# ScalarE's order in the first feed-forward projection: the gate slab's split ahead of Silu

## The reference

```
def swiglu_ffn(h, w_in, w_out):            # h: 256 x 1024
    gate, up = jnp.split(h @ w_in, 2, axis=-1)     # w_in: 1024 x 5632
    return (jax.nn.silu(gate) * up) @ w_out        # w_out: 2816 x 1024

x = x + 0.5 * swiglu_ffn(rms_norm(x, gain), w_in, w_out)
```

## Time and profile before

| | |
|---|---|
| times of three runs, us | 2641.64, 2650.41, 2651.55 |
| span of the profiled execution, us | 2652.8 |
| mean granted clock of PE in it | 0.992 |
| PE busy | 2573.4 us, 97% |
| VectorE busy | 1748.1 us, 66% |
| ScalarE busy | 1318.0 us, 50% |
| moved by DMA | 424.27 MB, mean 160 GB/s |
| `lo` on VectorE (L347) | 728 of them, 936.0 us |
| `hi` on ScalarE (L339) | 728 of them, 784.8 us |
| Silu (L692) | 176 of them, 73.5 us |

### The profile page before, as it was taken

The page is one execution under the profiler, slowest core; times in us unless marked ns, Lnnn a source line. Parts: engine busy times, 40 slices in busy tenths (PEclk is TensorE's granted clock), DMA queues, the critical chain, the costliest instruction groups (busy, mean ns, idle before and its releaser), DMA issues.

```text
span 2652.8 us, 60759 instructions
## 1 busy us (share of the span) xinstructions
PE 2573.4 (97%) x23370; PEld 2508.3 (95%) x23370; DVE 1748.1 (66%) x2814; ACT 1318.0 (50%) x1974; POOL 74.6 (3%) x106
## 2 busy tenths in 40 slices
PE   8998998899999999999999999899999999999999
PEld 7997977899999999989999999899999999999999
DVE  5757566566656757767657757967667566665774
ACT  5544433355545546545535547455455455554653
POOL 0000342000000000000000000000000000000000
PEclk9999999999999999999999999999999999999999
DMA  5654201344555655445654655236656564552564
GB/s 193 202 194 134 96 3 42 112 150 152 194 192 174 204 192 204 146 143 176 201 178 144 210 175 192 73 113 204 205 173 201 191 181 131 151 144 88 190 206 143
DMA packets 114323, 424.27 MB, mean 160 GB/s; under 512 B 12433, under 2 KB 19044, under 8 KB 113796
## 3 DMA queue, kind: packets, MB, share of 16 engines
q1 hardware_dynamic: 105696, 408.99, 46.3%
q10 hardware_dynamic: 8484, 13.30, 2.4%
HBM read 421.12 MB, written 1.12 MB: 159 GB/s over the span
## 4 chain that ended last, share of the span: by engine, by line
PE 91%; DVE 4%; ACT 2%; issue 1%; DMA 0%; ACTq 0%; POOL 0%; SPq 0%; DVEq 0%; POOLq 0%
PE bank L470 21%; PE bank L471 21%; PE bank L472 21%; PE bank L396 5%; PE bank L398 4%; PE bank L397 4%; PE bank L2268 2%; PE bank L1684 1%; PE bank L1659 1%; ACT hi L339 1%; PE bank L451 1%; PE bank L452 1%; PE bank L453 1%; PE bank L1230 1%; PE bank L1668 1%
## 5 line engine op out<-in xcount | busy, mean ns | idle before, releaser
L347 DVE TENSOR_TENSOR lo<-raw,hi 128x1024 fp32r<-128x1024 f32 (+1 forms) x728 | 936.0, 1294 | 396.7 <-ACT hi L339 395.2
L339 ACT ACTIVATE hi<-raw 128x1024 fp32r<-128x1024 f32 (+1 forms) x728 | 784.8, 1106 | 338.9 <-PE bank L398 194.5
L470 PE MATMUL bank<-Hh,hi 128*128 128x256 f32 x3056 | 849.5, 278 | 4.6 <-DVE lo L347 4.5
L471 PE MATMUL bank<-Hl,hi 128*128 128x256 f32 x3056 | 848.8, 278 | 0.0
L472 PE MATMUL bank<-Hh,lo 128*128 128x256 f32 x3056 | 848.7, 278 | 0.0
L470 PEld LDWEIGHTS bank<-Hh,hi 128*128 128x128 f32 x3056 | 577.8, 189 | 6.7 <-DVE lo L347 5.7
L471 PEld LDWEIGHTS bank<-Hl,hi 128*128 128x128 f32 x3056 | 574.7, 188 | 0.0
L472 PEld LDWEIGHTS bank<-Hh,lo 128*128 128x128 f32 x3056 | 574.5, 188 | 0.0
L471 PE MATMUL bank<-Al,hi 128*128 128x256 f32 x1408 | 390.5, 277 | 0.0
L472 PE MATMUL bank<-Ah,lo 128*128 128x256 f32 x1408 | 390.5, 277 | 0.0
L470 PE MATMUL bank<-Ah,hi 128*128 128x256 f32 x1408 | 390.4, 277 | 0.0
(11 more groups left out here) (418 smaller groups left out, 4158.7 us busy)
## 6 DMA issues: line engine op xcount, KB each, us to landing
raw<-in_w SPq DMA_DIRECT2D x600, 512.0 KB, 3.4
raw<-in_w SPq DMA_DIRECT2D x128, 704.0 KB, 4.3
dB<-dil_bias ACTq DMA_DIRECT2D x16, 384.0 KB, 9.4
X<-in_x SPq DMA_DIRECT2D x2, 512.0 KB, 5.4
mem_x<-in_mem ACTq DMA_DIRECT2D x1, 1024.0 KB, 5.0
gWS<-in_ws ACTq DMA_DIRECT2D x1, 1024.0 KB
gBS<-in_bs ACTq DMA_DIRECT2D x1, 1024.0 KB
out_x<-X SPq DMA_DIRECT2D x4, 256.0 KB, 2.6
```

What stands on the lines that cost most here:

```text
L339: act.activation(k.hi[:, q, :w], k.raw[:, q, :w], ACT.Copy).then_inc(k.hi_ready, 1)
L347: dve.tensor_tensor(k.lo[:, q, :w], k.raw[:, q, :w], k.hi[:, q, :w].bitcast(F32), ALU.subtract).then_inc(k.lo_ready, 1)
L470: pe.matmul(out, wh, xh, start=first, stop=False)
L471: pe.matmul(out, wh, xl, start=False, stop=False)
```

## The change

In ScalarE's order of a pair, the split of the next gate slab stands ahead of the waits for the scaled gate, and so ahead of Silu. Its own waits (the slab has landed, PE is through with the buffer) go with it. No other engine's order is touched.

```
                 turn = st.base // RING + i + 1
+                sh.act_hi(act, s + RING, 2 * j, ahead, turn)
                 act.wait_ge(k.gate_scaled, g + 1)
                 act.wait_ge(k.a_ready, g + 1)
                 act.activation(k.sgate[:, j, :], k.gate[:, j, :], ACT.Silu).then_inc(k.silu_done, 1)
-                sh.act_hi(act, s + RING, 2 * j, ahead, turn)
                 sh.act_hi(act, s + 1 + RING, 2 * j + 1, ahead, turn)
                 act.wait_ge(k.a_ready, g + 3)
```

## The result

| | kernel before | changed kernel |
|---|---|---|
| median of 15 runs each, us | 2655.34 (2641.64 to 2668.72) | 2666.07 (2657.12 to 2677.36) |
| ratio | | 1.0043, 95% interval 1.0024 to 1.0062 |
| span of the profiled execution, us | 2652.8 | 2662.3 |
| mean granted clock in it | 0.992 | 0.989 |

In these 30 runs the changed kernel is 0.2 to 0.6% slower; 0.3% was forecast. The kernel before was timed again in each of four later sessions.

The account below looks back on a forecast made before the run. PE, busy 97% of the span, was taken as the bound. Stall -1.5, clock -1.7, small waits -0.9 and paces +11.6 sum to +7.5 us: 2652.8 becomes 2660.3 profiled, 2658 as median, range 2643 to 2667.

Parts of the forecast that it names:

- the second case: Stage 0 draws the slow pace after its 0.74 us wait, paces carried: another 6.7 us, 2664.5; chance 0.17.
- The stall: PE's wait ahead of slab 4 in stage 0 shrinks by 1.51 us, from 2.25 to 0.74 us.
- Rival (d): ScalarE stays idle behind its table load, so stage 0's wait shrinks by only 0.32 us: 2649 to 2661; chance 0.04.
- The clock: Behind stage 0's wait, the half-speed stretch from about 34.9 to 38.3 goes: 1.7 us won.
- Later pairs: After a stage's first pair, VectorE's turn falls from 5.26 to 3.75 us, under PE's 5.44; nothing lost.
- The small waits: PE's waits at slab 4 of stages 1 to 7 vanish: 0.9 us won.
- The paces: Without waits at slab 4, feed-forward blocks keep the pace their norm gave, 276 or 281 ns per matmul: +11.6 us.
- The toggle: The norm matmuls in a stage's first pair of slabs switch PE between 276 and 281 ns, without an exception.
- rival (b): Paces carried, and stage 0 draws the slow one after its 0.74 us wait: another 6.7 us, 2664.5; chance 0.17.
- rival (c): Paces carried, but draws at waits upstream (1181, 1403, 2469 us) fall otherwise, one or two blocks quicker: 2651 or 2644; chance 0.14.
- The baseline: Two of the eight feed-forward blocks of the kernel before run slow, at 0.1178 us per matmul; median 2650.4 us.
- Rival (a): Pace isn't carried, or is drawn evenly at unseen places, so only the waits count: 2646 us; chance 0.23.

Follow-up runs that it names:

- run 3: New order in all pairs of each stage but the first, against the kernel before: 2656.53 against 2658.02 us, ratio 0.9987.
- run 1: The kernel before, unchanged, profiled once more: one execution 2669 us, median of 29 runs 2658 us.
- run 8: Kernel before with the new order in stage 0 only and one extra float32 matmul behind slab 7 there: 2668.23 us, ratio 0.9992.
- run 10: The kernel before, unchanged, profiled a third time in the last session: 2672.54 us (23 runs).
- run 2: New order in the first pair of each stage alone, against the kernel before: 2669.89 against 2658.02 us, ratio 1.0054.
- run 4: Changed kernel with one more float32 matmul ahead of slab 4 in stages 1 to 7: 2663.36 us, ratio to the kernel before 1.0035.
- run 7: Changed kernel with one extra float32 matmul in each of stages 0, 2, 4 and 7: 2663.33 us, ratio to the kernel before 0.9962.
- run 12: Changed kernel with extra float32 matmuls in stages 0, 2, 4 and 7, timed again: 2656.56 us, ratio to the kernel before 0.9941.
- run 6: Changed kernel, stages 1 to 7: PE waits for itself ahead of slab 4, then one float32 matmul: 2673.23 us, ratio to the kernel before 1.0034.

## Why the prediction was right, and where it wasn't

The direction, the size and the mechanism came out in the session of the result: forecast +7.5 us in the profiled pair, measured +9.5; median forecast 2658, measured 2666, just inside the range and near the second case's 2664.5. Of the 8 us between these medians 4.9 are the kernel before's own: its median was 2650.4 in three runs and 2655.3 in 15. That +7.5 came so near to +9.5 is partly luck, as the parts show.

- **The stall**: -1.51 forecast, -1.51 measured (34.35 to 32.84). The drain behind the table load that the Trainium skill has (ScalarE: Activation LUTs, What ACT_TABLE_LOAD costs) isn't there: the split starts at 30.05, 0.01 us behind the load's end at 30.04. Rival (d) is out by the same line.
- **The clock**: full speed from 34.95 to 38.30, as forecast, and 1.5 us there where 1.7 was forecast. Over the 14 profiles a half-speed stretch followed the stall in two of four with 2.25 us of waiting and in none of ten with 0.7 us. It bought nothing that the span shows. Elsewhere the changed kernel lost some 6 us in and beside half-speed stretches (0.989 against 0.992 on the mean), a part that the sum doesn't have; the drops differ from execution to execution.
- **Later pairs cost nothing**: shown by run 3, within its interval. VectorE's turn of 3.75 us was exact.
- **The small waits** are gone in stages 1 to 7: the steps to slab 4's first matmul are 0.9 us shorter together, as worked out, and the steps behind it another 0.4.
- **The paces**: +11.6 us forecast, +7.9 measured. The eight blocks gave +13.1 of the 13.4 forecast, and the streams between them -5.2 where -1.8 was forecast. These 3.7 us less and the clock's 6 us more offset each other in part, and that is the luck in the sum.
- **The toggle** held at twelve norms of each of the 14 profiles, 168 of 168. The other four of each profile (27.6, 206.4, 490.1 and 1394.2 in the profile before) have idle matmuls or other kinds of matmuls behind them, and no toggle can be read there: the "without an exception" of the prediction covers the streams.
- **The term that went the other way** is stage 0. I let it draw quick; behind the 0.7 us wait it came slow in 9 of 10 profiles, behind the 2.25 us one in 1 of 4. That is 6.5 us in the profiled pair, rival (b), to which I gave 0.17. It was hidden there, since the upstream draws, as in rival (c), went one block the other way: stages 5, 6 and 7 were slow, quick, quick instead of quick, slow, slow. The count of four slow blocks was the forecast's, the places were not; that it agreed is luck.
- **The baseline**: I took two slow blocks for the kernel before's own. Three more profiles with its waits had three, three and four, and its median in other sessions was up to 17 us higher. Its lead of 0.4% goes with sessions in which its draws at slab 4 fell well (13 of 21 quick in the profiles of the earlier trace rows, runs 1 and 3); in the last two sessions (5 of 14 quick in runs 8 and 10) there was no lead. Five profiles are few for that, and it is argued from them rather than shown. What the 14 profiles do show is that the paces make most of the spread between executions: the spans differ by 33 us, and less 4.5 ns for each step at the slow pace (6726 to 11864 of them, steps of 116 to 120 ns) by 12. A forecast of the mean over sessions would have been nearer to no change.
- Rival (a), that no pace is carried, is out by runs 2 and 4. The Trainium skill (TensorE: Matmul & The Clock Gate, Back-to-back issue gap) gives about 81 ns at 128 columns and 131 ns at 512 for a stream of weight loads and matmuls, and nothing for 256; its N/2.4 + 2.5 ns, 109 ns at 256, is for an isolated matmul. It has no second pace, and 113.3 and 117.8 ns are neither's number.

What the paces are inside PE stays open, and so does why stage 0 falls slow behind the shorter wait.

## What to carry to other kernels

When one engine is busy for 97%, look at the start-to-start step of its instructions and not at its waits alone: here 4.5 ns in a step of 113 is 6.7 us in one block, more than the 3.2 us that PE waited at slab 4 in all eight stages of the kernel before. A small wait that a change removes may have been doing something else, so compare the stages on both sides of it before it is counted as a gain. When two times differ by less than a kernel's own spread over chips, time both in several sessions, on other chips, and let a profile say which term moved.

## What the runs showed of the hardware that I had not expected

- A stream of weight load and 128x128x256 matmul pairs has two paces at full clock, 113.3 and 117.8 ns, and keeps one for up to 186 us over loops and stages.
- A float32 matmul (two records each in the trace) in the running stream switches to the other pace: 184 of 184, the 168 norms, seven in run 4 and nine in runs 7, 8 and 12. Right behind a wait it doesn't (7 of 7 in run 6).
- A wait of PE for its own semaphore leaves the pace (7 of 7, idle 0.34 to 0.44 us). A wait ended by VectorE changes it or not (22 of the table's 30 did); what decides is open.
- The same kernel's median differed by 17 us over five sessions, 0.6%, while another order of the same instructions moved by 2.4 us over three.
